# Norm weights folded into the split of the residual tiles, and the low parts of weights on GpSimd only in the feed-forward layers

## What is computed

```python
def rmsnorm(x, g):
    y = x * lax.rsqrt(jnp.mean(x * x, axis=-1, keepdims=True) + EPS)
    return y * g
...
h = h + mixer(rmsnorm(h, norm_mix_g), w_in, w_out)
h = h + cross_attention(rmsnorm(h, norm_x_g), mem, w_q, w_kv, w_o)
h = h + (jax.nn.silu(rmsnorm(h, norm_ffn_g) @ w_gate) * (rmsnorm(h, norm_ffn_g) @ w_up)) @ w_down
```

## Time and profile before

| | |
|---|---|
| median of 3 executions | 1401.49 us (1399.77 to 1406.76) |
| profiled execution, its own time | 1400.34 us |
| span in the profile | 1398.5 us |
| PE busy / DVE / ACT / POOL | 1296.8 / 860.2 / 683.9 / 257.1 us |
| POOL's low parts of weights | 99, of which 33 outside the feed-forward nets |

### The profile page before, as it was taken

How to read it: one execution, slowest core, us unless ns; L and a number is a source line. 1 busy time by engine, 2 the same in 40 slices (tenths; PEclk the granted TensorE clock), 3 DMA queues, 4 the chain that set the end, 5 groups by cost and what they waited for, 6 DMA issues and landing times.

```text
span 1398.5 us, 23028 instructions
## 1 busy us (share of the span) xinstructions
PE 1296.8 (93%) x9136; PEld 1173.7 (84%) x9136; DVE 860.2 (62%) x1575; ACT 683.9 (49%) x1197; POOL 257.1 (18%) x160
## 2 busy tenths in 40 slices
PE   7999899898999999898898899999999996999997
PEld 6777689798999999797658589999896584899996
DVE  2999666563654444655427477777744466777775
ACT  3442534554544444634525555555635445655554
POOL 5000000021222222122002022222222010222221
PEclk9999999899999999999759799999999999999999
DMA  7333323142465555244004155555454032455551
GB/s 307 106 98 113 106 91 106 61 145 97 152 195 182 183 182 186 99 166 151 0 7 145 32 167 186 185 185 182 150 182 137 1 106 73 133 187 182 181 181 46
DMA packets 51226, 187.91 MB, mean 134 GB/s; under 512 B 5680, under 2 KB 5808, under 8 KB 50736
## 3 DMA queue, kind: packets, MB, share of 16 engines
q1 hardware_dynamic: 51120, 186.44, 40.8%
HBM read 185.37 MB, written 1.05 MB: 133 GB/s over the span
## 4 chain that ended last, share of the span: by engine, by line
PE 77%; DVE 10%; ACT 7%; issue 4%; DMA 1%; POOL 0%; SPq 0%; DVEq 0%; ACTq 0%
PE banks L352 55%; PE banks L382 4%; PE banks L728 4%; PE banks L685 2%; ACT w_hi L857 2%; PE banks L708 2%; DVE a_lo L1320 1%; PE banks L422 1%; DVE h L1653 1%; PE banks L405 1%; PE banks L546 1%; DVE w_lo L1299 1%; ACT arena L1159 1%; PE banks L475 1%; PE banks L556 1%
## 5 line engine op out<-in xcount | busy, mean ns | idle before, releaser
L1948 POOL TENSOR_TENSOR w_lo<-w_raw,w_hi 128x1024 fp32r<-128x1024 f32 x99 | 238.1, 2405 | 1115.3 <-ACT w_hi L857 1115.3
L857 ACT ACTIVATE w_hi<-w_raw 128x1024 fp32r<-128x1024 f32 x313 | 328.9, 1051 | 197.5 <-PE banks L352 190.9
L352 PE MATMUL banks<-a_hi,w_hi 128*128 128x256 f32 x1432 | 411.9, 288 | 13.6 <-DVE a_lo L1320 5.5
L352 PE MATMUL banks<-a_lo,w_hi 128*128 128x256 f32 x1432 | 406.5, 284 | 0.0
L352 PE MATMUL banks<-a_hi,w_lo 128*128 128x256 f32 x1432 | 406.3, 284 | 0.0
L1299 DVE TENSOR_TENSOR w_lo<-w_raw,w_hi 128x1024 fp32r<-128x1024 f32 x214 | 262.0, 1224 | 88.0 <-ACT w_hi L857 87.9
L352 PEld LDWEIGHTS banks<-a_hi,w_hi 128*128 128x128 f32 x1432 | 276.3, 193 | 21.1 <-DVE a_lo L1320 11.7
L352 PE MATMUL banks<-b_hi,w_hi 128*128 128x256 f32 x880 | 257.0, 292 | 21.6 <-DVE h L1653 6.7
L352 PEld LDWEIGHTS banks<-a_lo,w_hi 128*128 128x128 f32 x1432 | 276.3, 193 | 0.3
L352 PEld LDWEIGHTS banks<-a_hi,w_lo 128*128 128x128 f32 x1432 | 276.1, 193 | 0.0
L352 PE MATMUL banks<-b_lo,w_hi 128*128 128x256 f32 x880 | 252.8, 287 | 0.0
(11 more groups left out here) (325 smaller groups left out, 1542.9 us busy)
## 6 DMA issues: line engine op xcount, KB each, us to landing
w_raw<-in_weights SPq DMA_DIRECT2D x342, 512.0 KB, 3.5
h<-in_x SPq DMA_DIRECT2D x1, 1024.0 KB, 4.9
arena<-in_mem SPq DMA_DIRECT2D x1, 1024.0 KB, 13.3
early<-in_mem SPq DMA_DIRECT2D x1, 1024.0 KB, 14.9
out_h<-h SPq DMA_DIRECT2D x2, 512.0 KB, 2.7
cons<-in_cons SPq DMA_DIRECT2D x1, 962.0 KB, 7.9
arena<-in_late SPq DMA_DIRECT2D x1, 448.0 KB, 4.2
pars<-in_pars SPq DMA_DIRECT2D x1, 290.5 KB, 2.9
```

The source lines that it names most:

```text
L352: ins = mm(out, l, r, start=start and n == 0, stop=stop and n == 2, skip_group_check=check)
L857: do(WHI[:, n % SPLIT_SLOTS, :], RAW[:, n % RAW_SLOTS, :], ACT.Copy).then_inc(*inc("w_hi_made", ("w_hi", n)))
L1948: g.tensor_tensor(WLO[:, n % SPLIT_SLOTS, :], RAW[:, n % RAW_SLOTS, :], WHI[:, n % SPLIT_SLOTS, :].bitcast(F32), ALU.subtract).then_inc(*i ...
```

## The change

Three edits. `gain` and the tiles `HG` are gone: ACT makes the high part of the scaled tile from `H` with the norm's weights as its scale (`hi_gained`), and DVE multiplies and subtracts in one instruction (`lo_gained`). ACT now makes the high part ahead of the square, and DVE the low part of tile m - 1 ahead of the sum of squares. `whole_mean_square` moves on PE from ahead of tile 7's matmuls to behind the first product. `lo_on_pool` is false outside the feed-forward nets.

```diff
@@ lo_on_pool
             return (s - FIRST[name]) % 3 == 2
-    return s % 3 == 0
+    return False
@@ build
-        HG = sb("gained", [P, 2, T])
@@ PE: fm, and the same in ffn after f == 0 and g == 0
+                if m == 0 and whole_sum:
+                    whole_mean_square(whole_sum)
...
-                fm("x_q", m, A, lambda k: ("a_lo", "xa", k), lambda k: whole_mean_square("xa", k))
+                fm("x_q", m, A, lambda k: ("a_lo", "xa", k), whole_sum="xa")
@@ ACT
+            def hi_gained(tag, m, x, src, g, ready):
+                act.wait_ge(*at(ready))
+                do(x[0][:, m, :], src, ACT.Copy, scale=par(g, m)).then_inc(*inc("input_hi", ("a_hi", tag, m)))
@@ ACT residual
                     ahead(FIRST[name] + (m * K + K - 1) // 8)
+                    hi_gained(tag, m, A, H[:, m, :], g, ("h", tag, m))
                     square(tag, m, H[:, m, :], ("h", tag, m))
-                    hi(tag, m, A, HG[:, m % 2, :], ("hg", tag, m))
@@ ACT ffn
                 for m in range(KD):
+                    if g_next:
+                        hi_gained(tag_next, m, A, H[:, m, :], g_next, ("h", tag_next, m))
                     if tag_next == "mx0":
                         square("fin1", m, H[:, m, :], ("h", tag_next, m))
                         square("mx0", m, H[:, m, :], ("h", tag_next, m), par("g_fin", m))
                     else:
                         square(tag_next, m, H[:, m, :], ("h", tag_next, m))
-                    if tag_next != "fin2":
-                        hi(tag_next, m, A, HG[:, m % 2, :], ("hg", tag_next, m))
@@ DVE
-            def gain(tag, m, src, g, ready=None):
-
-                if ready:
-                    dve.wait_ge(*at(ready))
-                if ("hg_used", tag, m) in hg_before:
-                    dve.wait_ge(*at(hg_before["hg_used", tag, m]))
-                v.tensor_scalar(HG[:, m % 2, :], src, par(g, m), None, ALU.mult).then_inc(
-                    *inc("gained", ("hg", tag, m)))
+            def lo_gained(tag, m, x, src, g):
+                dve.wait_ge(*at(("a_hi", tag, m)))
+                v.scalar_tensor_tensor(x[1][:, m, :], src, par(g, m), x[0][:, m, :].bitcast(F32),
+                                       ALU.mult, ALU.subtract).then_inc(*inc("input_lo", ("a_lo", tag, m)))
@@ DVE residual
                     step(v.tensor_tensor(H[:, m, :], H[:, m, :], acc_bank(t), ALU.add),
                          ("h", tag, m), ("acc", t), label="h_made")
-                    gain(tag, m, H[:, m, :], g)
                     if m:
+                        lo_gained(tag, m - 1, A, H[:, m - 1, :], g)
                         square_sum(tag, m - 1)
-                        lo(tag, m - 1, A, HG[:, (m - 1) % 2, :])
+                lo_gained(tag, KD - 1, A, H[:, KD - 1, :], g)
                 square_sum(tag, KD - 1)
-                lo(tag, KD - 1, A, HG[:, (KD - 1) % 2, :])
@@ DVE ffn
-                    if g_next:
-                        gain(tag_next, m, H[:, m, :], g_next)
-                        if m:
-                            lo(tag_next, m - 1, A, HG[:, (m - 1) % 2, :])
+                    if g_next and m:
+                        lo_gained(tag_next, m - 1, A, H[:, m - 1, :], g_next)
                 if g_next:
-                    lo(tag_next, KD - 1, A, HG[:, (KD - 1) % 2, :])
+                    lo_gained(tag_next, KD - 1, A, H[:, KD - 1, :], g_next)
```

More of the change, by code:

```diff
@@ L363, in raw, with fm @@
                 return RAW[:, s % RAW_SLOTS, b * P:(b + n) * P]
-            def fm(name, m, x, x_ready, sums=None):
+            def fm(name, m, x, x_ready, sums=None, whole_sum=None):
                 K = SHAPE[name][0]
@@ L752, in ffn @@
                             s += 1
+                            if f == 0 and g == 0:
+                                whole_mean_square(tag)
                     if f:
@@ L820, in _ @@
             for m in range(2):
-                fm("m_q0", m, A, lambda k: ("a_lo", "xa0", k), lambda k: whole_mean_square("xa0", k))
+                fm("m_q0", m, A, lambda k: ("a_lo", "xa0", k), whole_sum="xa0")
             attention("xa0", 4, 64, QF, KM[:, 0, :, :], VM[:, 0, :, :], False)
@@ L1183, in values_hi, with ffn @@
                     *inc("values_hi", ("o_hi", tag, grp)))
-            residual("w_out", "xa")
+            residual("w_out", "xa", "g_x")
             plain("x_q")
             attention("xa", 4, 256, False)
-            residual("x_o", "f0")
-            def ffn(name, tag, tag_next, conv=None):
+            residual("x_o", "f0", "g_ffn")
+            def ffn(name, tag, tag_next, g_next, conv=None):
                 silu_set()
@@ L1226, in ffn @@
                 rstd("fin1" if tag_next == "mx0" else tag_next, MR1 if tag_next == "mx0" else R)
-            ffn("ffn0", "f0", "mx0")
+            ffn("ffn0", "f0", "mx0", "g_both")
             act.wait_ge(*at("mx0_arg"))
@@ L1261, in _ @@
             attention("moba", 8, 64, True, 4)
-            residual("ab_o", "xa0")
+            residual("ab_o", "xa0", "g2_xa0")
             plain("m_q0")
             attention("xa0", 4, 64, False)
-            residual("m_o0", "f1")
-            ffn("ffn1", "f1", "mx1", conv=0)
+            residual("m_o0", "f1", "g2_ffn0")
+            ffn("ffn1", "f1", "mx1", "g2_mix1", conv=0)
             plain("fox_q")
@@ L1280, in _ @@
             attention("fox", 16, 64, True)
-            residual("fox_o", "xa1")
+            residual("fox_o", "xa1", "g2_xa1")
             plain("m_q1")
             attention("xa1", 4, 64, False)
-            residual("m_o1", "f2")
-            ffn("ffn2", "f2", "fin2", conv=1)
+            residual("m_o1", "f2", "g2_ffn1")
+            ffn("ffn2", "f2", "fin2", None, conv=1)
         @block.vector
@@ L2036 @@
     _reader[_buf] = _sum if _t not in SUMMED or _m == 0 else ("ssq", _t, _m)
-_tags = ["xa", "f0", "mx0", "xa0", "f1", "mx1", "xa1", "f2"]
-_seq = [(t, m) for t in _tags for m in range(KD)]
-for _i, (_t, _m) in enumerate(_seq):
-    if _i >= 2:
-        hg_before["hg_used", _t, _m] = ("a_lo", *_seq[_i - 2])
 def fm_blocks(w):
```

11 lines of the change are left out of this document (4 added, 7 removed).

## The result

| | before | changed |
|---|---|---|
| median | 1402.91 us (1399.77 to 1441.75, 22 executions) | 1418.31 us (1400.85 to 1439.29, 22 executions) |
| profiled execution, its own time | 1400.34 us | 1418.7 us |
| span | 1398.5 us | 1416.9 us |
| mean granted clock of PE | 0.961 | 0.940 |
| PE busy | 1296.8 us | 1320.1 us |

The ratio is 1.0049, with a 95% interval of [1.0025, 1.0073]: half a per cent slower, where 0.3% faster was predicted (1396.7 against 1401.49). The ratios in this text leave out executions more than 1.5% above the fastest of their kernel, which the medians include. The 22 executions of the changed kernel form three groups, and the granted clock goes with them: nine of 1400.85 to 1406.99 us (clock 0.948 to 0.954), seven of 1417.37 to 1420.20 (0.938 to 0.941), six of 1438.76 to 1439.29 (0.922 to 0.925). Of the kernel before, 21 of 22 are at 1399.77 to 1410.08.

What follows compares the result with a forecast made beforehand. PE bounds the nets; at eight seams it waits for DVE and ACT. Terms summed to -4.8 us from the profiled 1400.34, giving 1395.5, or 1396.7 for the median; 80% range 1391.5 to 1401.

Steps and rivals of the forecast that it cites:

- `w_out` and `x_o`, turns and tail: Two 8-slot seams: lost POOL help and stalls cancel, a_hi with a scale costs 0.03 us per turn, `w_out` tail -0.1; +0.3.
- `ab_o`, turns: 8-slot seam `ab_o`: help and stall cancel to 0, a_hi with a scale costs 0.03 us per turn; +0.2.
- `fox_o`, first addition to the first product of small attention 1: 8-slot seam `fox_o`: last addition 1.94 us later, most regained from a stalled a_lo, +0.5; with a_hi's cost +0.7.
- `m_o0` and `m_o1`: Seams paced by DVE: turn falls from 1.39 to 1.18 us without the gain, about -1.1 each, -2.2 together.
- end of `ffn0`: First a_hi about 1.0 us sooner, and PE's own 1.21 us per tile sets the pace instead of 1.44; -1.95.
- end of `ffn1`: PE's 0.79 us per tile sets the pace instead of 1.02, and the start comes 0.2 us sooner; -1.8.
- rotation stall and projections: Low parts moved to DVE stay hidden in the projections, and PE's 0.76 us wait for a stalled rotation goes; -0.8.
- `glu`: The low part of slot 48 on DVE delays a copy PE waits for by 1.2 us, 0.5 of it slack; +0.75.
- A: The forecast itself, over the whole kernel: a gain of 3 to 7 us, likeliest median 1396.7 us; chance 0.57.
- B: More comes back: shorter 3.38 us turns and seam tails, `ffn0` at its bound; -9.4 us, 1392; chance 0.22.
- C: Savings at nets and `m_o` seams swallowed by the chain of table load, `R` and first activation; -0.8, 1400.7; chance 0.14.
- D: a_lo stalls stay without POOL's parts, 1407.5 us; milder form, a_lo meets POOL's third slot, 1403; both together 0.07.

Runs made afterwards that it cites:

- e1_fold_only: The changed kernel with POOL keeping its 33 low parts outside the nets, so the fold alone: median 1417.39 us, ratio 0.9948.
- the filler: Four overwritten 128x128 bf16 matmuls on PE ahead of each 64-wide head's scores; added to the changed kernel: median 1397.20 us, later 1396.64; to the kernel before: 1396.97.
- e0_again: The changed kernel run once more with nothing altered: median 1405.63 us, ratio 1.0003; its profiled execution took 1438.80 us.
- g0_before_shift1: The kernel before with three products of `ffn1` computed three times more, 1.1 us of PE work: median 1434.76 us, ratio 1.0085.
- g2_fold_shift2: The fold alone, POOL's low parts kept, with three products of `ffn1` computed seven times more, 2.5 us: median 1392.98 us, ratio 0.9940.

## Why the prediction was wrong

The step that failed is a term that the sum doesn't have: it took every stage between the seams as it was, 0 us, without a reason, and no rival touched them. The prediction named the clock only in its last sentence, "if PE's clock at the seams differs from before". It was the clock in the attentions between the seams that moved: +20.3 us in the profiled execution, 13.0 of them in the forgetting attention.

**The terms of the sum**, measured as distances in the two profiled executions:

| term | predicted | measured |
|---|---|---|
| `w_out` and `x_o`, turns and tail | +0.3 | +0.2 |
| `ab_o`, turns | +0.2 | +0.5 |
| `fox_o`, first addition to the first product of small attention 1 (30.23, then 30.86) | +0.7 | +0.6 |
| `m_o0` and `m_o1` (10.70 and 10.79, then 9.63 twice) | -2.2 | -2.2 |
| end of `ffn0` (last addition of `x_o` to the end of PE's wait for `R`: 210.89, then 210.03) | -1.95 | -0.9 |
| end of `ffn1` (7.66, then 5.72) | -1.8 | -1.9 |
| rotation stall and projections (from there to stick breaking: 71.39, then 70.38) | -0.8 | -1.0 |
| `glu` (last corrections to the first addition of `w_out`: 21.56, then 22.10) | +0.75 | +0.5 |
| sum | -4.8 | -4.2 |
| stages of attention, the same work at a lower clock | 0 | +20.3 |
| rest (start up to `glu` +1.1, tail of `ab_o` +0.6, others) | 0 | +2.3 |

The rows above the sum were right in sign, and all but one within 0.3 us. The end of `ffn0` was mis-sized. DVE's additions there do come closer, 8.10 us for all eight against 10.90, after a start 1.3 us later. But PE's tiles are 1.36 us apart, not 1.21: ACT's three operations (0.49, 0.42 and 0.51, started 1.36 from one a_hi to the next) are the pace, where the prediction had PE's own. PE's wait behind this seam, before and then in the changed kernel, shows what passes on:

```profile
586.79 0.58 PE L352 MATMUL banks<-a_hi,w_hi 128*128 128x256 f32 x1 [4.82 <-DVE arena L1438]
```

```profile
587.74 0.58 PE L351 MATMUL banks<-a_hi,w_hi 128*128 128x256 f32 x1 [4.85 <-DVE arena L1438]
```

From the last additions of `x_o` (375.90, then 377.71) these are 210.89 and 210.03 us. The wait of 0.76 us ahead of the rotation product is gone from the changed kernel's trace. In `glu` the copy starts 3.61 us after the last corrections against 2.38, so 1.23 later, as predicted, and 0.5 of it reaches the first addition of `w_out` (22.05 to 22.11 us in the four profiled executions with the changed kernel's `glu` and seams, 21.56 in the two of the kernel before).

Executions of before and after at one mean clock differ by 1 to 5 us in the predicted direction (at 0.956: 1404.94 to 1405.59 and 1400.5; at 0.950 to 0.951: 1406.53 to 1409.13 and 1405.40 to 1405.83). That agrees with the sum, though a mean clock says nothing of where it was low.

**The rivals.** A, the work of the forecast, is what the seams show. B fell: the turn stayed at 3.39. C fell: small attention 1 began as counted. D fell for the changed kernel, no a_lo is long; but e1_fold_only shows that the milder form of D is real, a fused a_lo stalls when it meets POOL. None of the four had the clock in it. The range, 1391.5 to 1401.0, would have held one of the 22 executions, 1400.85.

**The sign by halves.** The fold is the gain: with POOL kept and, in the profiled execution, full clock in the forgetting attention it took 1392.98 us, 9.4 below the kernel before measured beside it, the 2.5 us of useless products included. Moving the low parts costs 5 to 7 us with the fold (lowest executions 1399.16 and 1400.85 against 1393.86), and up to 12 without it (1411.93 against 1399.77). The four seams with 8 slots say why. From first to last addition they take 92.65 us together in the kernel before, 88.34 in e1_fold_only, 95.57 in the changed kernel, and 94.60 when only the low parts move. So the fold alone saves 4.3 us in turns for which the prediction had +0.8, and the moved parts take back 7.2, against 2.0 without the fold. "Help and stall cancelled" was true of the kernel before and not with the fold: it takes away the stalled gains, though not the stalled a_lo, and what is left of POOL is more help than stall. The prediction costed the two edits as one.

**What is shown and what is argued.** Shown: the terms of the seams; that the 20.3 us lost in the attentions go with a lower granted clock at unchanged work of DVE and ACT, 13.0 of them with 30.7 us of half clock in the forgetting attention; that 1.1 us more of the same work brings the drop into the kernel before, and that 2.5 us more take it out of the profiled executions of the changed kernel and of the fold alone, and the upper group out of all six of the fold. Argued: that in the changed kernel it was the 2.4 us (276.46 to 274.08), most of them saved in `ffn1`, that brought the attention to its bad place; with 2.5 us given back the profiled execution kept the clock and the group near 1418 was gone, but not the one at 1439. Open: why one place keeps the clock and the next loses it, and what the filler changes in that; why the clock is lower in stick breaking and MoBA (3.7 us) and in small attention 1 (3.6 us), also in the profile with 2.5 us more, where they are 3.7 and 3.0 us longer; and why three executions with 2.5 us more are at 1439 and above.

## What to carry to other kernels

Where PE runs long stages of small products, write the granted clock of each stage beside its time before a small gain is forecast, and give the forecast a case in which a stage that was at full clock is not: here it was worth 13.0 us (69.20 against 56.18) or 32.9 (89.03), against a sum of 5. Judge such a change by the groups of its executions and by stages at the same clock, not by one median. And when an edit removes the cost of a helper's interference, ask again whether the helper should stay.

## What the hardware showed that was not expected

In the forgetting attention PE is busy for 30.70 of 30.70 us by the profile and stays at half clock (0.50) all that time; e0_again, e1_fold_only and g0_before_shift1 did so for 85.30 us, with 82.51 busy. The page "TensorE: Matmul & The Clock Gate" of the Trainium skill (section "HAM oscillation — how this bites in real kernels") describes a clock that falls when PE waits between groups of matmuls; here it fell 2.4 us after a stage began in which no wait of PE is seen before the drop (2.42 busy of 2.42). One wait of 0.94 us stands just ahead of the stage, but it stands there in the kernel before too, which kept the clock. So busy time as the profile models it does not tell whether the clock will hold. The same page of the Trainium skill says that the chip's check runs free of the kernel's start (Part 1, "What's actually happening"). With that agrees that one program has executions with and without the drop, and that the place behind the last half-clock stretch sorts the eight profiles without filler.

A low part of weights on DVE is stretched by POOL too: in g2_fold_shift2 the one that starts at 298.93, with POOL at work until 299.86, took 2.01 us against the mean of 1.22. The additions into `h`, which read a PSUM bank, were not: 6 in the kernel before and 8 in e1_fold_only overlap POOL, and none takes over 0.43 us.
